# A normalisation factor's load moved from the sync engine's DMA queue to the head of ScalarE's

## The reference, cut to what matters

```python
def rmsnorm(x, g, eps=EPS):
    xf = x.astype(jnp.float32)
    y = xf * lax.rsqrt(jnp.mean(xf * xf, axis=-1, keepdims=True) + eps)
    return (y * g.astype(jnp.float32)).astype(x.dtype)
...
        u = rmsnorm(h, g_pre_mix[i])
        proj = u @ w_in[i]
```

## Time and profile before

| what | us |
|---|---|
| median of 3 runs | 924.96 |
| lowest and highest of them | 924.56, 925.87 |
| span of the profiled execution | 925.7 |
| TensorE busy | 900.7 |
| VectorE, ScalarE, POOL busy | 453.8, 396.4, 369.5 |
| mean granted TensorE clock, share of full speed | 0.995 |

### The profile page before, as it was taken

How to read it: one execution, slowest core, us unless ns; L and a number is a source line. 1 busy time by engine, 2 the same in 40 slices (tenths; PEclk the granted TensorE clock), 3 DMA queues, 4 the chain that set the end, 5 groups by cost and what they waited for, 6 DMA issues and landing times.

```text
span 925.7 us, 12765 instructions
## 1 busy us (share of the span) xinstructions
PE 900.7 (97%) x4327; PEld 742.3 (80%) x4327; DVE 453.8 (49%) x887; ACT 396.4 (43%) x700; POOL 369.5 (40%) x195
## 2 busy tenths in 40 slices
PE   7999999999999999999999999999999999999997
PEld 6877777877787778788888779888888888888886
DVE  4677786665566562353334155655555555400004
ACT  4455445566555563434333144534443444312112
POOL 4333223322222332754455454544444444444441
PEclk9999999999999999999999999999999999999999
DMA  7431133221222210433333721433333332323202
GB/s 226 128 112 45 46 90 91 72 73 59 63 63 75 74 58 24 137 101 92 90 92 113 241 77 47 137 91 91 106 97 91 92 107 95 113 102 103 91 23 92
DMA packets 132140, 86.13 MB, mean 93 GB/s; under 512 B 6822, under 2 KB 121454, under 8 KB 132098
## 3 DMA queue, kind: packets, MB, share of 16 engines
q1 hardware_dynamic: 131050, 81.86, 29.5%
q10 hardware_dynamic: 1048, 3.72, 1.2%
HBM read 83.42 MB, written 2.14 MB: 92 GB/s over the span
## 4 chain that ended last, share of the span: by engine, by line
PE 86%; DVE 8%; ACT 2%; issue 2%; DMA 1%; POOL 0%; ACTq 0%; DVEq 0%; SPq 0%; POOLq 0%
PE banks L1220 26%; PE banks L1222 26%; PE banks L1221 26%; PE banks L1363 3%; PE banks L1295 2%; PE banks L1294 2%; DVE lam_ratio L1045 1%; DMA wide<-in_g_pre_mix_dram 1%; PE banks L1239 1%; DVE pages L942 1%; ACT pages L657 1%; DVE scratch L878 1%; DVE pages L937 1%; DVE scratch L1020 1%; ACT pages L623 0%
## 5 line engine op out<-in xcount | busy, mean ns | idle before, releaser
L518 POOL TENSOR_TENSOR ring_lo<-ring_raw,ring_hi 128x1024 fp32r<-128x1024 f32 x142 | 343.8, 2423 | 499.0 <-ACT ring_hi L615 498.8
L1220 PE MATMUL banks<-u_hi,ring_hi 128*128 128x512 f32 (+1 forms) x800 | 310.3, 388 | 0.0
L1222 PE MATMUL banks<-u_hi,ring_lo 128*128 128x512 f32 (+1 forms) x800 | 305.6, 382 | 0.0
L1221 PE MATMUL banks<-u_lo,ring_hi 128*128 128x512 f32 (+1 forms) x800 | 305.1, 381 | 0.0
L615 ACT CAST ring_hi<-ring_raw 128x1024 fp32r<-128x1024 f32 x142 | 147.7, 1043 | 133.4 <-PE banks L1222 125.3
L1222 PEld LDWEIGHTS banks<-u_hi,ring_lo 128*128 128x128 f32 x800 | 150.7, 188 | 29.5
L1220 PEld LDWEIGHTS banks<-u_hi,ring_hi 128*128 128x128 f32 x800 | 151.0, 189 | 27.5 <-DVE u_lo L884 0.2
L1221 PEld LDWEIGHTS banks<-u_lo,ring_hi 128*128 128x128 f32 x800 | 151.0, 189 | 27.5
L1185 DVE SCALAR_TENSOR_TENSOR wide<-banks,cols,wide 128x511 f32<-128x511 f32 x88 | 65.9, 749 | 87.4 <-ACT wide L837 80.6
L1220 PE MATMUL banks<-ring_hi,pages 128*128 128x512 f32 x240 | 93.8, 391 | 1.7 <-DVE scratch L1118 1.6
L1221 PE MATMUL banks<-ring_lo,pages 128*128 128x512 f32 x240 | 93.4, 389 | 0.0
(11 more groups left out here) (134 smaller groups left out, 1051.1 us busy)
## 6 DMA issues: line engine op xcount, KB each, us to landing
ring_raw<-in_w_ffn_up_dram SPq DMA_DIRECT2D x88, 256.0 KB, 3.1
ring_raw<-in_w_in_dram SPq DMA_DIRECT2D x60, 256.0 KB, 3.3
ring_raw<-in_w_gate_dram SPq DMA_DIRECT2D x48, 256.0 KB, 3.1
ring_raw<-in_w_ffn_down_dram SPq DMA_DIRECT2D x44, 256.0 KB, 2.7
ring_raw<-in_w_out_dram SPq DMA_DIRECT2D x16, 256.0 KB, 2.9
scratch<-in_x_dram SPq DMA_DIRECT2D x4, 512.0 KB, 6.5
ring_raw<-in_w_proj_a_dram SPq DMA_DIRECT2D x8, 256.0 KB, 2.7
ring_raw<-in_w_proj_c_dram SPq DMA_DIRECT2D x8, 256.0 KB, 3.0
```

The lines of the kernel that those rows point to most:

```text
L518: pool.tensor_tensor(wlo[:, r, :], raw[:, r, :], whi[:, r, :].bitcast(F32), ALU.subtract).then_inc(w_lo_done, 1)
L1220: pe.matmul(out, lhs_hi, rhs_hi, start=start, stop=False)
L1221: pe.matmul(out, lhs_hi, rhs_lo, start=False, stop=False)
L1222: return pe.matmul(out, lhs_lo, rhs_hi, start=False, stop=stop)
```

## The change

The load of g_pre leaves SP's stream, where it stood behind x tiles 0 and 1, and becomes the first instruction of ScalarE's stream. Source, destination, size and the semaphore that VectorE waits for stay.

```diff
             load_x(0)
             load_x(1)
-            sp.dma_start(g_pre, g_pre_mix[0].partition_broadcast(P)).then_inc(small_loaded[2], 16)
 
             def load_small():
...
+            act.dma_start(g_pre, g_pre_mix[0].partition_broadcast(P)).then_inc(small_loaded[2], 16)
             act.wait_ge(x_loaded[0], 16)
             square(0, 0, x_tok[:, 0, :])
```

## The result

The change made the kernel slower. Nine runs of the changed kernel have a median of 928.87 us; the kernel before, now also with nine runs, has 927.0 us, and not the 924.96 us of its first three. One of those nine, of 999.15 us, fell in a slower state of the chip and is left out of the comparison, which takes the other eight; they have a median of 926.4 us. The ratio of the runs is 1.0033, with a 95% interval of 1.0022 to 1.0044: some 3.1 us more, with 2.0 to 4.1 us possible.

A forecast was written before the change was run, and what follows sets the result against it. The prediction took TensorE, busy for 97% of the span, to bound the kernel, with the start's chain feeding it. Gains of 0.61 and 0.7 us sum to 1.3 us: 923.7 us against 924.96, range 922.4 to 925.4.

The forecast's parts named there:

- Where the change acts: Start of the kernel: what moves the u_hi 1 cast at 13.28 moves the rest and the end with it.
- First term: u_hi 1 on ScalarE no longer waits for TensorE and can start at 12.67, not 13.28: 0.61 us gained.
- VectorE's promised 2.4 us: VectorE's first two scalings, without the wait for g_pre, run 2.4 us earlier; ScalarE doesn't let that gain through.
- Second term: Weight tile 0 lands earlier as g_pre moves beside the x tiles: 0.7 us, about half the 1.5 us upper bound.
- x beside g_pre: x tiles 0 and 1, sharing with g_pre, land up to 1.4 us later; cost nothing, cover 0.5 us at worst.
- stays: At tile 3, VectorE's scaling still collides with POOL's subtraction and takes 3.38 us, not 1.3; both shift together.
- tile 1 is turned by 12.2 even at the half clock: TensorE finishes turning token tile 1 before 12.67, even with x late, so it doesn't delay u_hi 1.
- named for "wrong": Weight tile 0 later than 10.7, x tile 1 after 8, or clock 0.50 at the turning of tile 3.
- signs for "right": Among others: first scaling starts at 6.3 to 7.7, released by POOL; u_hi 1 follows u_hi 0 unwaited, near 12.
- rival 3: TensorE's half clock falls on the first products and lasts to turning tile 3: +0.9 us, 925.9, or 927.5; chance 0.10.
- Rival 4: g_pre comes as late as now, held behind x on the shared engines: no change, 925.0; chance 0.05.
- Rival 1: g_pre's transfer time is not recovered for the weight tile: only 0.61 us gained, 924.4; chance 0.22.

The follow-up runs named there:

- experiments 2 and 3: Changed kernel with the rows of x tile 3 loaded instead of g_pre: ratio 1.0020; the same with POOL made to wait for VectorE's second scaling: 1.0008.
- Experiment 1: Changed kernel with POOL made to wait for VectorE's second scaling before its subtraction for weight tile 0: ratio 1.0010 to the kernel before.
- Experiment 4: Changed kernel with g_pre as first transfer on SP's own queue, ahead of the x tiles, nothing on ScalarE's: ratio 1.0033 to the kernel before.
- experiments 6, 9 and 10: Kernel before with POOL held for VectorE's fourth scaling: 0.9981; that with 40 warming transposes, not 28: 0.9982; the first with table transposes moved after token tile 3's turning: 0.9978.

## Why the prediction was wrong

- **Where the change acts**: right. u_hi 1 sets the chain, and everything behind it shifted as one (2.80 us at u_hi 1, 2.79 at the first scores, 2.8 in the span). What the time does beyond that depends on where TensorE's clock falls, as the table shows.
- **First term, 0.61 us**: its premise, that VectorE's promised 2.4 us would stop at ScalarE's wait for weights, never came into play. VectorE's own chain became the later one.
- **Second term, 0.7 us by an earlier weight tile**: the cast moved from 10.71 to 9.42, 1.3 us, inside the bounds of 0 and 1.5. It gained nothing, as TensorE's turning came last, and it helped to do harm: with weight tile 0 rounded by 10.46, POOL had its subtraction ready at the moment its second rstd was done. A row bore on this term and was not weighed: beside the broadcast that landed 4.6 us after its issue on ScalarE's queue, the same view has two more such broadcasts that took far longer, and the prediction names only the fastest of the three.

```profile
wide<-in_g_post_mix_dram ACTq DMA_DIRECT2D x1, 512.0 KB, 8.3
wide<-in_g_pre_ffn_dram ACTq DMA_DIRECT2D x1, 512.0 KB, 9.1
```

- **The step that failed is "x beside g_pre: cost nothing, cover 0.5 us".** Its size was wrong first: 1.4 us as the upper end, 2.27 and 2.20 us measured. It took only the bytes at full rate (experiments 2 and 3: 1.6 to 1.8 us already with ordinary rows) and left out the slow repeated row (0.5 to 0.6 us more), although the paragraph on the weight tile had the 144 GB/s in hand. Where g_pre's slow reads end up was asked for the weights, and not for x. Worse, what follows x was taken over unchanged: rstd 1 some 2.06 us after x tile 1 was ready, and the scaling at 1.28 us. Both went wrong because VectorE and POOL now met. POOL's norm_ms 1 took 1.06 us instead of 0.19; it started 0.27 us into VectorE's first scaling and ended 0.05 us behind it. The second scaling took 3.35 us behind POOL's subtraction.
- **The bill.** The forecast had u_hi 1 at 12.67 - 0.7 = 11.97 us; it came at 16.08, 4.11 us later. An estimate from the rows: had both engines kept their own lengths, rstd 1 would have come at 7.56 + 2.20 = 9.76, the second scaling would have started at 9.94, right behind the first, and u_hi 1 at about 13.28, as before. So x's lateness alone would have eaten the forecast gain of 1.3 us and no more. norm_ms's wait put the second scaling to 10.66, 0.71 us behind the 9.95 it had in the kernel before, and the collision added 3.35 - 1.28 = 2.07 us. Experiment 1 shows the last item; no run took away norm_ms's wait.
- The very same collision stood in the prediction, at tile 3, with its rows, and was called a thing that "stays". It was not asked whether the shift makes a new one at tile 1, where POOL's subtraction follows rstd 1 in POOL's program and only the late weight tile had kept it 1.9 us away (11.83 against 9.95).
- **Clock**: "tile 1 is turned by 12.2 even at the half clock" failed with the scaling, whose end came at 14.01. TensorE's pauses became 3.67 and 2.98 us, not under 1.3.
- **The signs** that were named for "wrong" didn't come: weight tile 0 came before 10.7, x tile 1 was ready at 7.70, ahead of the 8 us named, and the clock at the turning of tile 3 was full. By the step's own cover, 0.5 us beyond the 1.4, the limit for x tile 1 was 7.4 us, and that one was passed. Two signs for "right" did fail: the first scaling started at 8.66, and u_hi 1 waited 3.94 us behind u_hi 0.
- **Rivals**: rival 3, the clock, had the sign but not the mechanism of the changed kernel; its price of 2.2 us is close to the 2.1 us that the half clock cost in experiments 1 and 3. Rival 4, no gain, had the chain closer than the forecast. No rival had x landing late with the path behind it on VectorE and POOL. Rival 1 rested on the Trainium skill's rule ("DMA: Bandwidth & Descriptors", section "Issuing engines are not separate DMA queues") that several issuing engines save only issue time. Experiment 4 agrees, with the same ratio of 1.0033 from SP's queue; but the second term was not zero for that, as weight tile 0 was rounded 1.3 us earlier.
- **The base**: 924.96 us was the median of three runs and lay low; with more runs beside it the kernel before had 926.2 to 927.1. About 2 us of the distance between 923.7 and 928.87 are this. In ratio the forecast was 0.9986 and the result 1.0033.

## What to carry to other kernels

Before a transfer is moved forward, list what it is moved past or beside, and follow each of those to its own consumers: here two 512 KB tiles that everything starts with paid for one that nobody needed before rstd was ready. Whenever a start time shifts on VectorE or POOL, look up which instructions of the two now become ready within the same microsecond, small ones too; in these runs VectorE's scaling and a POOL instruction that reads SBUF never ran side by side, and the one that started second paid for the rest of the first. A wait that puts them in the right order can be worth more than the change itself.

Judge a step of 1 or 2 us by many runs and by the chain, and not by one profile's span: here single executions of one kernel lie as far apart as the change moved the median. The kernel before took 924.2 us on average where its mean granted clock was 0.998, and 927.5 us where it was 0.993.

## What the runs showed of the hardware that was not expected

- VectorE's scaling, which has two SBUF inputs, and POOL's subtraction do not overlap at all: where the scaling starts 0.01 to 0.07 us behind a subtraction of 2.34 to 2.37 us it takes 3.35 to 3.41 us, and alone 1.28 us, in every profile. It goes the other way too: POOL's 128x1 norm_ms takes 0.19 us alone and 1.01 to 1.16 us beside a scaling. VectorE's `u_lo`, whose other input is in PSUM, is not held: it takes its usual 1.23 us in the middle of a subtraction that ran from 11.83 to 14.20.

```profile
12.70 1.23 DVE L884 TENSOR_TENSOR u_lo<-banks,u_hi 128x1024 fp32r<-128x1024 f32 x1 [1.48 <-ACT u_hi L627]
```

  The Trainium skill ("SBUF — State Buffer", section "Who interferes with whom") says so: a VectorE instruction with two SBUF inputs contends with a GpSimd one that reads SBUF, and the second to issue waits for the whole of the first. The runs agree.
- 512 KB of ordinary rows on the second queue delay the first x tile by 1.6 to 1.8 us. By the Trainium skill's turns between queue rows ("DMA: Bandwidth & Descriptors", section "Queues, rings and completion order") an estimate is the other transfer's time, 1.4 us for 512 KB at 383 GB/s; the runs are a little above it.
- The same 512 KB broadcast takes 4.4 us to land when first on SP's queue, 5.5 when first on ScalarE's beside x, 7.0 as third on SP's, and 7.5 when issued on an empty ScalarE queue at 4.26 us. A queue of its own was no shortcut past what the other queue had outstanding.
- The kernel before doesn't start alike each time: with the same loads in the same order, g_pre let the first scaling start at 8.74, 7.87, 8.15 and 8.52 us (the kernel before, experiments 6, 9 and 10).
